# A hybrid decoder step on one core: the samples' small attention steps set beside the page groups

## The reference, cut to what matters

```python
for l in range(DEPTH):
    shared = (g_pre[l], w_in[l], g_qa[l], w_uq[l], ...)
    # prompt: projections, MLA over itself, GLA, memory attention, merge with w_out
    ...
    (q, ckv, kpe, gate_mla, gq, gk, gv, gg, gate_gla, mq, gate_mem) = _branch_inputs(xs, pos_s, *shared)
    lat = _mla_sample(q, ckv, kpe, pos_s, cache_ckv, cache_kpe, page_table, l, w_uk[l], g_mla_k[l])
    gla_o, s_fin = _gla_chunked(gq, gk, gv, gg, state_gla[l])
    mem_o = _mem_attn(mq, cache_mem_k[l], cache_mem_v[l])
    xs = _merge(xs, lat, w_uv[l], gate_mla, gla_o, g_gla_o[l], gate_gla, mem_o, gate_mem, w_out[l])

def _mla_sample(...):           # online softmax: a page at a time, then the new tokens
    carry, _ = lax.scan(page_step, init, (page_table.T, jnp.arange(n_pages)))
    k_new = _mla_keys(c_new, kpe_new, pos_new, w_uk, g_k)
    sc = jnp.where(causal, einsum(q, k_new) * MLA_SCALE, NEG_INF)
    m, l, acc = _online_update(carry, sc, c_new)
    return acc / l
```

## Time and profile before

| what | value |
|---|---|
| median of 3 runs | 3263.43 us (3263.2 to 3265.43) |
| the profiled execution | 3262.92 us, its span 3261.1 us |
| mean granted TensorE clock | 0.954 |
| instructions | 56019 |

### The profile page before, as it was taken

The page is one execution under the profiler, slowest core; times in us unless marked ns, Lnnn a source line. Parts: engine busy times, 40 slices in busy tenths (PEclk is TensorE's granted clock), DMA queues, the critical chain, the costliest instruction groups (busy, mean ns, idle before and its releaser), DMA issues.

```text
span 3261.1 us, 56019 instructions
## 1 busy us (share of the span) xinstructions
PE 3063.3 (94%) x20312; PEld 1892.1 (58%) x20312; DVE 1593.1 (49%) x3500; ACT 1029.6 (32%) x2145; POOL 328.4 (10%) x469
## 2 busy tenths in 40 slices
PE   6999999977999999997979999999779999999989
PEld 4666666655555555554446666666545555555544
DVE  3565555534555555551135655655345555555511
ACT  1333333311444444440013323333114444444400
POOL 1100100101111111110011000001011111111000
PEclk9999999976999999997989999999769999999989
DMA  5000000012122222214420000001121222222122
GB/s 223 15 16 16 29 18 13 29 39 73 49 56 59 59 55 55 56 54 143 163 103 15 16 24 22 16 13 40 28 73 51 55 58 59 57 56 54 54 99 91
DMA packets 196905, 179.53 MB, mean 55 GB/s; under 512 B 98547, under 2 KB 176406, under 8 KB 194582
## 3 DMA queue, kind: packets, MB, share of 16 engines
q1 hardware_dynamic: 196630, 175.95, 17.8%
HBM read 153.90 MB, written 21.97 MB: 54 GB/s over the span
## 4 chain that ended last, share of the span: by engine, by line
PE 79%; DVE 13%; ACT 3%; issue 2%; POOL 2%; DMA 1%; SPq 1%; DVEq 0%; ACTq 0%
PE ps L1577 28%; PE ps L1262 11%; PE ps L1691 6%; PE ps L1591 4%; PE ps L1564 4%; PE ps L1604 3%; PE ps L1424 3%; PE ps L1256 2%; PE ps L1438 2%; PE ps L1267 2%; PE ps L1593 2%; POOL rs L485 2%; ACT U L586 1%; PE ps L1287 1%; PE ps L1414 1%
## 5 line engine op out<-in xcount | busy, mean ns | idle before, releaser
L1156 DVE TENSOR_REDUCE W<-mkv 128x8 f32<-128x512 f32 x512 | 351.2, 686 | 577.2 <-ACT mkv L707 572.3
L1577 PE MATMUL ps<-w_uk,region 128*128 128x512 f32 x1248 | 587.6, 598 | 1.3
L1262 PE MATMUL ps<-w_in,xT 128*128 128x256 f32 (+9 forms) x2016 | 568.6, 436 | 1.9 <-DVE xT L820 1.9
L1262 PEld LDWEIGHTS ps<-w_in,xT 128*128 128x128 f32 (+1 forms) x2016 | 368.2, 187 | 163.0 <-issue 75.5
L1577 PE MATMUL ps<-w_uk,xT 128*128 128x512 f32 x800 | 375.6, 597 | 1.1 <-ACT mkv L707 0.5
L707 ACT ACTIVATE mkv<-ps 128x512 f32<-128x512 f32 x512 | 305.7, 597 | 175.2 <-PE ps L1577 150.2
L1577 PEld LDWEIGHTS ps<-w_uk,region 128*128 128x128 f32 x1248 | 216.2, 191 | 196.4 <-issue 191.8
L485 POOL TENSOR_TENSOR rs<-us,mhalf 128x1 f32<-128x1 f32 (+5 forms) x134 | 132.2, 986 | 1348.6 <-DVE us L841 632.7
L1577 PEld LDWEIGHTS ps<-w_uk,xT 128*128 128x128 f32 x800 | 138.3, 190 | 125.2 <-issue 122.8
L1564 PEld LDWEIGHTS ps<-ident,region 128*128 128x128 f32 x1024 | 124.3, 142 | 127.9 <-issue 123.4
L1564 PE MATMUL ps<-ident,region 128*128 128x128 f32 x1024 | 158.7, 278 | 2.8 <-DVE ws L1143 2.8
(11 more groups left out here) (354 smaller groups left out, 3996.8 us busy)
## 6 DMA issues: line engine op xcount, KB each, us to landing
region<-in_cache_ckv SPq DMA_DIRECT2D x512, 128.0 KB, 2.0
w_in<-in_w_in SPq DMA_DIRECT2D x16, 1240.0 KB, 10.6
mix_rows<-xn SPq DMA_DIRECT2D x16, 512.0 KB, 2.9
region<-in_cache_kpe SPq DMA_DIRECT2D x512, 16.0 KB, 1.8
region<-in_w_out SPq DMA_DIRECT2D x8, 1024.0 KB
xt<-in_x_prompt SPq DMA_DIRECT2D x12, 512.0 KB, 5.1
xt<-x_mid SPq DMA_DIRECT2D x12, 512.0 KB, 4.6
region<-in_w_mem_kv SPq DMA_DIRECT2D x2, 2048.0 KB, 10.1
```

The lines of the kernel that those rows point to most:

```text
L1156: tell(dve.tensor_reduce(pst[:, 0, j * H:j * H + H], heads(sqb[:, j % 2, :], H), X, ALU.add), s.pkn_red, np_)
L1262: ins = mm(out, xT[:, k, 0:T], w_in[:, k, c0:c0 + w], start=k == 0, stop=k == KD - 1)
L1577: ins = mm(ps[:, 2 + j % 2, :], page[:, o_:o_ + P], w_uk[:, c, :], start=c == 0, stop=c == 1)
```

## The change

The samples' steps are cut into 31 small ones a layer. In each page group, ahead of the work for page j, each of the three compute engines calls its `sample_step(k, j)`, which holds the step for that place: the key weights and queries turned and absorbed in k = 0, the new tokens' scores, weights and values in k = 1 and the first half of k = 2, the gates in k = 3, linear attention in k = 4 and its states in k = 5 to 8, a sequence's memory keys turned in each of k = 9 to 16, memory scores, softmax and values in k = 17 and 18, the last transposes in k = 19.

Their buffers (`scratch`) lie in `w_in`, no longer in `region`. The page groups' tables move (`cosp` to `xn`, `sinp` to `mkv`), so that a page group and the samples' steps can be under way together. Scores of pages use bank 4 only; bank 5 is the small steps'. The new tokens' scores are computed for a sequence's own eight tokens only (8 moving columns, 24 products), with rows (head, token) on the partitions, and the maxima are those of a row of that layout, without transposes and without a product that spreads them; their mask comes from a small product at the start. The values take one masked matrix a sequence (`pz`). The memory scores are put with rows (sequence, head, token) on the partitions, in four strips of 32, so that the softmax is along a row; the transposed keys of all sequences are kept.

The gates are copied out of the two banks first (`gates_exp`) and worked on in k = 3. On SP's queue the first two groups' pages come ahead of the samples' memory and states, and the stores of states and rows come after the loads of k = 14 and 24. The sum of squares of the positional keys is reduced at j = 3, not ahead of j = 0.

The core of the diff:

```diff
+        cosp = xn[:, :].rearrange("p (j n) -> p j n", j=PAGES)
+        sinp = mkv[:, :, :].rearrange("p a n -> p (a n)").rearrange("p (j n) -> p j n", j=PAGES)
...
+        scratch = w_in[:, :, :].rearrange("p k n -> p (k n)")
+        smk = scratch[:, 0:4096].rearrange("p (b c n) -> p b c n", b=DB, c=2)
+        smv = scratch[:, 4096:8192].rearrange("p (b c n) -> p b c n", b=DB, c=2)
+        s_bd = scratch[:, 8192:10240].rearrange("p (b n) -> p b n", b=DB)
+        kdz = scratch[0:TS, 10240:11264].rearrange("p (b n) -> p b n", b=DB)
+        qz = scratch[:, 11264:11776].rearrange("p (b n) -> p b n", b=DB)
+        qz_own = scratch[:, 11264:11840].rearrange("p (b n) -> p b n", b=DB)[:, :, 0:DT]
+        ukT = scratch[:, 12032:13056].rearrange("p (h r) -> p h r", h=4)
+        sn, rT = scratch[0:TS, 13056:13120], scratch[0:TS, 13120:13184]
+        smkT = scratch[:, 10240:14336].rearrange("p (b c n) -> p b c n", b=DB, c=2)
+        mqz = scratch[:, 14336:14848].rearrange("p (c b n) -> p c b n", c=2, b=DB)
+        pz = scratch[0:TS, 14848:15360].rearrange("p (b n) -> p b n", b=DB)
...
+                        sp.wait_ge(s.o_ps, TP * (L + 1))
+                        sp.dma_start(sinp, a["c_sinp"]).then_inc(s.x_in, 16)
+                        load_pages(0)
...
+                sp.wait_ge(s.cT_ps, 2 * n + 2)
                 sp.dma_start(cosp, a["c_cosp"]).then_inc(s.x_in, 16)
+                load_pages(1)
+                sp.wait_ge(s.gates_ps, 2 * n + 2)
...
+                for k in range(2, DB * NG):
...
+                pool.wait_ge(s.gates_ps, 2 * n + 2)
+                pool.memset(s_bd, 0.0).then_inc(s.st_zero, 1)
...
+                    if t == TP:
+                        act.wait_ge(s.gates_ps, 2 * n + 2)
+                        tell(act.copy(gate[0:TS, :].rearrange("p (c n) -> p c n", c=2), ps[0:TS, 6:8, :]), s.gates_exp, n_gexp(n))
+                        break
...
+                    if k == 0 and j == 3:
+                        dve.wait_ge(s.qnT_ps, 2 * L + 2)
+                        own(cp(qnT, ps[:, 4, 0:256]))
+                        for q in range(4):
+                            w = slice(32 * q, 32 * q + 32)
+                            ins = cp(qrz[w, q, :].rearrange("p (b h n) -> p b h n", b=DB, h=H),
+                                     ps[w, 5, :].rearrange("p (h b n) -> p b h n", h=H, b=DB))
+                            if q < 3:
+                                own(ins)
+                        tell(ins, s.qnT_evac, L)
...
+                    if k == 1 and j == 3:
+                        dve.wait_ge(s.pnT_ps, L + 1)
+                        tell(tt(pz, over_heads(ps[0:TS, 5, 0:TS], TS, DB, TS), per_head(tokmask[:], TS, DB, TS), ALU.mult), s.pz_ready, L)
+                    if k == 1 and j >= 4 or k == 2 and j < 4:
+                        b = (j - 4) % 8
+                        dve.wait_ge(s.acc_ps, DB * L + b + 1)
+                        tell(cp(acc[0:TS, b, :], ps[0:TS, 5, 0:RW]), s.acc_ready, DB * L + b)
...
+                        sample_step(k, j)
+                        if j == 3:
+                            dve.wait_ge(s.kpe_rot, n0 + 1)
+                            tell(dve.tensor_reduce(kk[:, k % 2, :], rtmp[:, 1, :].rearrange("p (j n) -> p j n", j=G), X, ALU.add), s.kk_ready, n0)
...
+                def sample_step(k, j):
+
+                    n = NT * L + TP
+                    if k == 0 and j == 0:
+                        pe.wait_ge(s.am_ready, n + 1)
+                        pe.wait_ge(s.gates_exp, n_gexp(n) + 1)
+                        for hp in range(4):
+                            for c in range(2):
+                                o_ = (hp % 2) * 256 + c * P
+                                ins = tp(ps[:, 4 + hp // 2, o_:o_ + P], w_uk[:, c, hp * P:hp * P + P], ident[:])
+                        ins.then_inc(s.ukT_ps, 1)
+                    if k == 0 and j == 1:
+                        pe.wait_ge(s.qn_ready, L + 1)
+                        mm(ps[0:TS, 6, 0:TS], qk[0:TS, 1, 640:704], ident[0:TS, 0:TS], start=True, stop=True)
+                        tp(ps[:, 6, TS:2 * TS], qk[0:TS, 1, 512:640], ident[0:TS, 0:TS]).then_inc(s.qnT_ps, 1)
+                    if k == 0 and j == 2:
+                        pe.wait_ge(s.ukT_evac, L + 1)
+                        for c in range(4):
+                            tp(ps[:, 4, c * TS:c * TS + TS], qk[0:TS, 1, c * P:c * P + P], ident[0:TS, 0:TS])
+                        for h in range(H):
+                            ins = tp(ps[:, 5, h * TS:h * TS + TS], qrep[:, h * P:h * P + P], ident[0:TS, 0:TS])
+                        ins.then_inc(s.qnT_ps, 1)
+                    if k == 0 and j == 5:
+                        pe.wait_ge(s.qnT_evac, L + 1)
+                        for h in range(H):
+                            w = slice(NOPE * (h % 2), NOPE * (h % 2) + NOPE)
+                            for c in range(2):
+                                o_ = c * 256 + (h // 2) * TS
+                                ins = mm(ps[:, 4 + 2 * (h % 2), o_:o_ + TS], ukT[w, h // 2, c * P:c * P + P], qnT[w, (h // 2) * TS:(h // 2) * TS + TS], start=True, stop=True)
+                        ins.then_inc(s.qt_ps, 1)
+
+                    if k == 1 and j == 0:
+                        for b in range(DB):
+                            for c in range(3):
+                                at, of = (cT[:, c, DT * b:DT * b + DT], qt[:, c, 64 * b:64 * b + 64]) if c < 2 else (rk[:, DT * b:DT * b + DT], qrz[:, 0, 64 * b:64 * b + 64])
+                                ins = mm(ps[0:TS, 5, DT * b:DT * b + DT], of, at, start=c == 0, stop=c == 2)
+                        ins.then_inc(s.sn_ps, 1)
+                    if k == 1 and j == 2:
+                        pe.wait_ge(s.pn_ready, L + 1)
+                        tp(ps[0:TS, 5, 0:TS], sn, ident[0:TS, 0:TS]).then_inc(s.pnT_ps, 1)
+                    if k == 1 and j >= 4 or k == 2 and j < 4:
+                        b = (j - 4) % 8
+                        if b == 0:
+                            pe.wait_ge(s.pz_ready, L + 1)
+                        else:
+                            pe.wait_ge(s.acc_ready, DB * L + b)
+                        mm(ps[0:TS, 5, 0:RW], pz[:, b, :], ck[0:TS, :], start=True, stop=True).then_inc(s.acc_ps, 1)
+
+                    if k == 4 and j == 0:
+                        pe.wait_ge(s.acc_ready, DB * (L + 1))
+                        pe.wait_ge(s.kdz_ready, L + 1)
+                        pe.wait_ge(s.smk_in, 128 * (L + 1))
+                        for b in range(DB):
+                            mm(ps[0:TS, 5, 0:GW], qz[:, b, :], s_bd[:, b, :], start=b == 0, stop=False)
+                        for h in range(GH):
+                            ins = mm(ps[0:TS, 5, GV * h:GV * h + GV], am[0:TS, h, 0:TS], gvs[:, GV * h:GV * h + GV], start=False, stop=h == GH - 1)
+                        ins.then_inc(s.glao_ps, 1)
+                    if 5 <= k < 9 and j == 0:
+                        q = k - 5
+                        if q == 0:
+                            pe.wait_ge(s.go_ready, n + 1)
+                        else:
+                            pe.wait_ge(s.glas_ready, n_glas(n) + q)
+                        for e in range(2):
+                            ins = mm(ps[:, 5, e * GW:e * GW + GW], kdz[:, 2 * q + e, :], gvs, start=True, stop=True)
+                        ins.then_inc(s.glas_ps, 1)
+
+                    if 9 <= k < 9 + DB and j == 0:
+                        b = k - 9
+                        if b == 0:
+                            pe.wait_ge(s.glas_ready, n_glas(n) + 4)
+                        else:
+                            pe.wait_ge(s.smkT_evac, DB * L + b)
+                        for hp in range(2):
+                            for c in range(2):
+                                ins = tp(ps[:, 5, hp * NM + c * P:hp * NM + c * P + P], smk[:, b, c, hp * P:hp * P + P], ident[:])
+                        ins.then_inc(s.smkT_ps, 1)
+                    if k == 17 and j == 0:
+                        pe.wait_ge(s.smkT_evac, DB * (L + 1))
+                        for b in range(DB):
+                            w = slice(32 * (b % 4), 32 * (b % 4) + 32)
+                                ins = mm(ps[w, 5, NM * (b // 4):NM * (b // 4) + NM], mqz[:, hp, b, :], smkT[:, b, hp, :], start=hp == 0, stop=hp == 1)
+                        ins.then_inc(s.smq_ps, 1)
+                    if k == 18 and j == 0:
+                        pe.wait_ge(s.smp_ready, L + 1)
+                        for g in range(2):
+                            for c in range(2):
+                                o_ = 256 * g + P * c
+                                ins = tp(ps[:, 5, o_:o_ + P], smp[:, g, c * P:c * P + P], ident[:])
+                        ins.then_inc(s.smpT_ps, 1)
+                    if k == 18 and j == 4:
+                        pe.wait_ge(s.smpT_evac, L + 1)
+                        for hp in range(2):
+                            for b in range(DB):
```

(17 more changed lines are left out.)

505 lines of the change are left out of this document (220 added, 285 removed).

## The result

The kernel before took 3264.23 us (median of 4, 3263.2 to 3265.43), the changed one 3228.48 us (median of 4, 3228.0 to 3230.63): a ratio of 0.9892, interval 0.9874 to 0.9909. It is 1.1% faster, 36 us; 116 were forecast, and the time lies above the range.

What follows compares the result with a forecast made beforehand. TensorE's own instructions were taken to bound the page groups. Removing 207.9 us plus 3.6 and adding 95.4 (47.7 a layer) saves 116.1 us from 3262.92, giving 3147 us, with a range of 3115 to 3188.

Steps and rivals of the forecast that it cites:

- rival 4: Page groups' own period grows (later squares reduction, one score bank); with 2.5 us a group 3307 us; chance 0.04.
- VectorE's and ScalarE's own steps: Small steps on these engines in the page groups: covered by the free half of their time, cost nothing.
- The stretch removed: Between the projections' end and the first page turned, both layers: 207.9 us go as a stretch of their own.
- the slow first groups: First page groups of each layer now start at the full clock: 1.8 us a layer, 3.6 in all, saved.
- Instructions added: Small steps' instructions put on TensorE inside the page groups: 34.9 us a layer, each counting fully.
- memory scores: Memory attention's 32 score products: only the border between samples overlaps, 6.0 us a layer.
- Waits: TensorE waits for gates' copy 0.7, before the absorption 1.7, in group k = 1 1.9: 4.3 us a layer.
- The clock: TensorE's clock falls at the memory values of k = 18 alone: 4.9 us a layer.
- the changes of the array's shape: Some 12 TensorE steps a layer with 64 or 32 outputs pay 0.3 us each: 3.6 us a layer.
- 1 (cheaper steps): In the small steps, scores overlap well, the clock holds, drains hide: 24 us less, 3123 us; chance 0.15.
- 2 (a low clock in many groups): TensorE's clock falls in the first group and other steps' groups: 50 us more, 3197 us; chance 0.10.
- 3 (VectorE falls behind): Steps before page reductions hold squares and keys; 20 groups lose 1.2 us each: 48 more, 3195 us; chance 0.09.

Runs made afterwards that it cites:

- experiment 1: Changed kernel with the reduction of the positional keys' squares put back ahead of a group's first page: 3146.6 us, ratio 0.9641.
- experiment 2: Changed kernel, reduction still at j = 3, but GpSimd's rotation held back until the sixth page is reduced: 3170.01 us, ratio 0.9717.
- experiment 4: Kernel before the change with only the reduction of the positional keys' squares moved to j = 3: 3343.16 us, ratio 1.024.
- experiment 3: Changed kernel with the reduction back ahead of the group, but GpSimd's rotation waiting until the third page is reduced: 3155.43 us, ratio 0.9662.

## Why the prediction was wrong

**The step that failed** is in rival 4: "from the third page to the next group's second lie some 12 us", given as the reason why the reduction may come later, and with it "VectorE's and ScalarE's own steps (the free half of their time covers them)", priced at nothing. I had named the right line and the right place and priced a deadline that is not the near one. I asked when GpSimd would have to be done, and had 12 us. I did not ask what stands behind the reduction in VectorE's own queue: the fourth page, the maxima, then ScalarE's Exp, copy and square, and TensorE's keys, with a deadline of nothing. The free half of VectorE's time is no cover there. In the kernel before its idle time lies ahead of the page reductions (2.72 us in the earlier trace rows), where it waits for squares; from the third page's reduction to the end of the maxima it ran without a pause. The timelines of VectorE, ScalarE and TensorE in the kernel before:

```profile
1115.78 0.29 DVE L1184 TENSOR_REDUCE glw<-ps 128x1 f32<-128x128 f32 x1
...
1116.68 0.29 DVE L1189 TENSOR_SCALAR glw<-ident,glw 128x128 f32<-128x128 f32 x1
1117.06 0.20 ACT L718 ACTIVATE glw<-glw 128x1 f32<-128x1 f32 x1 [2.13 <-DVE glw L1189]
...
1117.91 1.26 ACT L707 ACTIVATE mkv<-ps 128x512 f32<-128x512 f32 x2
1118.65 1.96 PE L1577 MATMUL ps<-w_uk,xT 128*128 128x512 f32 x4
```

The first of the two squares takes some 0.6 us and so ends near 1118.52; the keys that need it start 0.13 us later, right behind TensorE's own instruction before them. Where TensorE does wait for this square, in the changed kernel, the same 0.13 us lie between (1306.42 to 1306.55). So the burst and TensorE's own path ended together, with no slack between them and no wait to be seen.

**The missing 82 us** are 1.32 us in each of some 60 groups: 0.45 the instruction, 0.87 the two that GpSimd held up (experiments 1, 2, 4). With them out, the time is 3146.6 us, and 3147 was forecast. That is partly luck, as the terms show:

- *The stretch removed*, 207.9 us and the slow first groups: as forecast. The first page is turned right behind the projections, at 680.91.
- *Instructions added.* Absorption 2.05 us in 1.9 forecast, new tokens' scores 2.75 in 2.8, linear attention 4.0 (k = 4 takes 25.37 us in experiment 1; forecast 3.6 and 0.5), states 1.05 in each of k = 5 to 8 (22.38 us, once 22.73; forecast 0.93). The *memory scores* were mis-sized: 6.0 forecast, 2.0 measured. TensorE's groups by form in the changed kernel:

```profile
L1605 PE MATMUL ps<-w_in 128*32 128x256 f32 x32 | 2.0, 384 | 0.0
```

  32 instructions, each 0.384 us long, done in 2.0 us. I let only the border between two samples overlap; samples of four strips that take turns every four instructions overlap almost wholly. The Trainium skill, TensorEngine Tiling (Array Packing), Theoretical Speedup, gives up to four times for 32 outputs; the prediction set it beside the 6.0 as 1.8 us, and the trace agrees with the page.
- *Waits*: gates 0.68 us (0.7), absorption 1.65 (1.7), masked matrix 1.44 (1.5), the next copy 0.7 (0.4) in the changed kernel. Near the forecast; these came from counting what stands in VectorE's queue ahead of the awaited instruction, which is the very count left out in rival 4. One was not forecast: k = 17 grew by 3.1 us (24.42 in experiment 1), 2.0 for the scores and 1.14 for a wait of the keys on ScalarE's square, at 1085.62, since ScalarE has the memory softmax's two Exps (L722) to do before it. So ScalarE's own steps were not all covered either.
- *The clock*: 4.9 us a layer were forecast at k = 18. The step took 11.2 us where 64 products at the full clock take 7.4 (four times 1.86), and four keys 3.76 for 1.96: 5.6 in the changed kernel, 3.4 and 5.0 in experiment 1. The forecast that it dips there alone was wrong: in the changed kernel it also fell at k = 0 and k = 1 of both layers (700 to 702 us, 0.50), 1.7 us each.
- *The sum*: in experiment 1 the groups took 41.3 and 46.4 us a layer more than before (728.5 and 733.2 against 687.2 and 686.8), 87.8 in all; 91.8 were forecast. The scores' 8 us too much (two layers) make up for 3.4 us of low clock in the second layer's first two groups, for the two unforeseen waits at k = 17 (2.3) and for smaller terms. What the changes of the array's shape cost (3.6 us a layer forecast) was not measured by itself.

**The rivals.** 1 (cheaper steps) was right on the scores and wrong on the clock. 2 (a low clock in many groups) came in two groups, not in most. 3 (VectorE falls behind) has the mechanism, a step ahead of a page's reduction that holds the square and the keys, but was priced for the 20 groups with a step. Those did not lose by it: k = 9 to 16 took 21.76 us once the reduction was back, 0.43 over the plain period for 0.5 of instructions. Only k = 17 did, by 1.14 us, and by ScalarE's steps, not VectorE's. 4 named the place, and its point of 1.8 us a group was near what came, 1.32. Its chance of 0.04 was too low by far, and so the range ended under the result.

## What to carry to other kernels

When an instruction moves in an engine's queue, take the deadline not only of the one who waits for it but of everything that now stands behind it: a wait of zero in the profile doesn't say that there is slack, so compare the releaser's end with the waiter's start. Keep GpSimd's instructions away from the moments at which VectorE's short instructions are on the path; a moved wait shifts GpSimd too. A long run of narrow products, where the clock fell in it, was better cut into pieces with wide ones between them, and an event better told after the copy that its waiter needs than after the last of a batch.

## What the hardware showed that I had not expected

**VectorE held up by GpSimd.** An instruction of one column took 0.67 us in place of 0.16, and one of 128 columns 0.64 in place of 0.29, when a GpSimd instruction was under way as they came. Over all groups of the changed kernel and of experiments 3 and 4 the instructions of the maxima that were held up ended at most 0.10 us after GpSimd's did. One that had begun 0.02 us before GpSimd's kept its time (experiment 3). The page reductions were not stretched: the one from 1302.09 to 1302.78 had GpSimd's 1302.19 to 1302.65 beside it and took 0.69. Nor did L1243 show any delay where it came with 0.05 us of a GpSimd instruction left, or with 0.15 left (experiment 3, 1314.21). The Trainium skill, SBUF — State Buffer, Who interferes with whom, says that a VectorE instruction with two inputs in SBUF contends with a GpSimd instruction that reads SBUF, that a `tensor_scalar` can too, that a `tensor_reduce` never does on trn2, and that the issue order decides who blocks. The rows agree on each of the four points, save that L1243 with so little left shows nothing. What they add is the size for short instructions: the whole duration becomes what is left of GpSimd's instruction and up to 0.1 us, here up to 0.7 us for 0.16 of work.

**The clock behind narrow products.** 64 products of 16 columns on end brought the granted clock from 1.00 to 0.50 and 16 at a time, with four keys between, did not; 48 products of 8 columns did in 15 of 18 layers. In one piece the 64 did so in all 14 layers of the seven kernels that have them so, and in four parts in none of four. What decides about the 48 stays open.
